# Hymba decoder layer on one core: copy the turned weights first in each step of the attention loop

## The reference

```python
# FoX, per head: scores with a forget term, causal
s = einsum('bqhd,bkhd->bhqk', q, k) * scale
s = s + cum_t[query] - cum_t[key]
a = softmax(where(kpos <= qpos, s, NEG))
o = einsum('bhqk,bkhd->bqhd', a, v)
# NSA: three branches; with 512 tokens all 8 blocks are selected, so the
# selected and the sliding-window branch are both plain causal attention
a = softmax(where(causal, q @ k.T * scale, NEG));  o = a @ v
# the branches are summed with the gates g
```

## Time and profile before

| what | value |
|---|---|
| device time, median of 3 runs | 1250.01 us (1247.60 to 1250.06) |
| the profiled execution: its own time | 1247.07 us |
| its span in the trace | 1245.3 us |
| outside the span | 1.8 us |
| prompt attention, first score to last output copy | 560.8 to 708.7 us |
| one cycle of four steps, NSA half | 9.95 us |
| one cycle of four steps, FoX half | 10.9 us |

### The profile page before, as it was taken

The page is one execution under the profiler, slowest core; times in us unless marked ns, Lnnn a source line. Parts: engine busy times, 40 slices in busy tenths (PEclk is TensorE's granted clock), DMA queues, the critical chain, the costliest instruction groups (busy, mean ns, idle before and its releaser), DMA issues.

```text
span 1245.3 us, 23642 instructions
## 1 busy us (share of the span) xinstructions
PE 1175.5 (94%) x9650; PEld 1079.6 (87%) x9650; DVE 534.9 (43%) x787; ACT 426.3 (34%) x740; POOL 135.6 (11%) x132
## 2 busy tenths in 40 slices
PE   8999999999999999999999756999999999999994
PEld 6999999999998799995655422888999999999994
DVE  4434332343333653545277645545434323343334
ACT  6222222232244632225265523444222212232332
POOL 0110100011111000322011100120110100011110
PEclk9999999999999999999999976999999999999997
DMA  6222223222123223226150062131322232232221
GB/s 270 102 88 81 86 79 108 102 102 75 69 88 110 85 97 143 69 78 217 51 172 2 3 187 102 35 102 35 102 91 78 77 102 96 99 102 77 76 85 69
DMA packets 46002, 117.95 MB, mean 95 GB/s; under 512 B 4154, under 2 KB 21818, under 8 KB 39874
## 3 DMA queue, kind: packets, MB, share of 16 engines
q1 hardware_dynamic: 42738, 110.95, 26.3%
q10 hardware_dynamic: 3184, 5.88, 1.2%
HBM read 110.93 MB, written 7.97 MB: 95 GB/s over the span
## 4 chain that ended last, share of the span: by engine, by line
PE 88%; DVE 7%; ACT 2%; issue 2%; DMA 1%; DVEq 0%; SPq 0%; ACTq 0%
PE ps L1328 75%; PE ps L1455 2%; PE ps L1472 2%; PE ps L1488 2%; PE ps L1503 1%; PE ps L1337 1%; DVE row_max L1077 1%; DVE UT L917 1%; DVE H L921 1%; DVE XL L897 1%; PE ps L1463 1%; PE ps L1630 1%; PE ps L1421 0%; DMA RAW<-in_w_gu 0%; DMA KW<-in_win_k 0%
## 5 line engine op out<-in xcount | busy, mean ns | idle before, releaser
L1328 PE MATMUL ps<-XH,WH 128*128 128x260 f32 x1904 | 389.1, 285 | 8.3 <-DVE XL L897 8.1
L1328 PE MATMUL ps<-XH,WL 128*128 128x260 f32 x1904 | 383.5, 283 | 0.0
L1328 PE MATMUL ps<-XL,WH 128*128 128x260 f32 x1904 | 382.8, 283 | 0.0
L409 ACT CAST WH<-RAW 128x1024 fp32r<-128x1024 f32 (+2 forms) x183 | 174.8, 956 | 530.7 <-PE ps L1328 526.1
L1328 PEld LDWEIGHTS ps<-XH,WH 128*128 128x128 f32 x1904 | 294.6, 188 | 15.0 <-DVE XL L897 12.1
L1328 PEld LDWEIGHTS ps<-XH,WL 128*128 128x128 f32 x1904 | 293.4, 188 | 0.0
L1328 PEld LDWEIGHTS ps<-XL,WH 128*128 128x128 f32 x1904 | 292.7, 188 | 0.0
L412 DVE TENSOR_TENSOR WL<-RAW,WH 128x1024 fp32r<-128x1024 f32 (+2 forms) x183 | 203.7, 1113 | 157.9 <-ACT WH L409 156.6
L1328 PE MATMUL ps<-UL,WH 128*128 128x260 f32 x704 | 141.9, 283 | 0.0
L1328 PE MATMUL ps<-UH,WL 128*128 128x260 f32 x704 | 141.5, 282 | 0.0
L1328 PE MATMUL ps<-UH,WH 128*128 128x260 f32 x704 | 141.3, 282 | 0.0
(11 more groups left out here) (233 smaller groups left out, 934.5 us busy)
## 6 DMA issues: line engine op xcount, KB each, us to landing
RAW<-in_w_gu SPq DMA_DIRECT2D x44, 1024.0 KB, 4.8
RAW<-in_w_down SPq DMA_DIRECT2D x16, 768.0 KB, 4.8
RAW<-in_w_in SPq DMA_DIRECT2D x11, 1024.0 KB, 4.8
RAW<-in_w_down SPq DMA_DIRECT2D x16, 640.0 KB, 4.3
KF<-in_fox_k SPq DMA_DIRECT2D x16, 256.0 KB, 4.4
VF<-in_fox_v SPq DMA_DIRECT2D x16, 256.0 KB, 5.4
RAW<-in_w_out SPq DMA_DIRECT2D x4, 1024.0 KB, 4.9
H<-in_x SPq DMA_DIRECT2D x4, 520.0 KB, 7.2
```

The source lines that it names most:

```text
L409: nc.scalar.copy(WH[:, par, 0:width], RAW[:, slot, j, 0:width]).then_inc(w_hi, 1)
L1328: q = nc.tensor.matmul(ps[:, 2 * slot + half, 0:HALF], w[:, par, cols], x[:, kt0 + kt, half * HALF:(half + 1) * HALF], start=first and kt ...
```

## The change

In every step m from 3 on, except step 14, the copy of the turned pair m-3 stands first: on VectorE before the maximum of pair m, on ScalarE before the exponentials of pair m. In step 14 it stays last, since the burst's results share its banks. No instruction is added or taken away, and TensorE, GpSimd and SyncE keep their order.

```diff
@@ ScalarE, attention() @@
                     if m == 2:
                         ropes_free()
+                    if m >= 3 and m != BURST_AT:
+                        turn_out(act, nc.scalar.copy, 2 * (m - 3) + 1, "att_odd_out")
                     if m < PAIRS:
                         act.wait_ge(sem("att_max"), m + 1)
...
-                    if m >= 3:
+                    if m == BURST_AT:
                         turn_out(act, nc.scalar.copy, 2 * (m - 3) + 1, "att_odd_out")
                     if tiles and m >= pairs_until(tiles[0]) + 4:
                         pair_out(tiles.pop(0))
@@ VectorE, attention() @@
                 for m in range(PAIRS + 3):
+                    if m >= 3 and m != BURST_AT:
+                        turn_out(dve, nc.vector.tensor_copy, 2 * (m - 3), "att_even_out")
                     if m < PAIRS:
                         v, W = 2 * m, P * (unit(2 * m)[3] + 1)
...
-                    if m >= 3:
+                    if m == BURST_AT:
                         turn_out(dve, nc.vector.tensor_copy, 2 * (m - 3), "att_even_out")
```

## The result

The changed kernel took 1235.12 us in the median of 4 runs (1234.73 to 1239.13), before 1250.03 us in 4 runs (1247.60 to 1251.20). The ratio on record is 0.9907 with a 95% interval of 0.9882 to 0.9931. It is an estimate over the executions and not the quotient of the two medians, which is 0.9881. That is 9.4 us by the ratio and 8.9 us by the medians. The change makes the kernel faster by 0.6 to 1.2%.

A forecast was written before the change was run, and what follows sets the result against it. TensorE, busy 94% of the span, was taken as the bound, stalling once per attention cycle for VectorE's copy. Gains of 6.6 and 0.9 us sum to 7.5 us off the 1250.01 us median: 1242.5 us, range 1238.5 to 1247.5.

The forecast's parts named there:

- The ring through S(3): Attention loop, steps with i = 3: S(1) comes 0.64 us earlier, taken as 0.60, 11 times, 6.6 us.
- The end of the loop: After the last S(3): VectorE copies ahead of the last two scalings, so the last T(3) starts 0.9 us earlier.
- Copy first in the other steps: Attention steps with i = 0, 1 and 2: later maxima cost nothing, hidden by the second score buffer; 0.8 to 1.5 us room.
- The clock at the start of the loop: First cycle of the attention loop: the slow clock holds at most 1.5 us, to be won or lost once more.
- After the attention: Stages behind the attention: what follows hangs on its end and moves with it; no gain of its own in the sum.
- The starting point: Whole kernel: the time counted from the three-run median of 1250.01 us, 2.9 us above the profiled execution.
- B: Rival, attention loop: slower hand-overs lengthen the ring, break-even at 0.13 us more for each of five; about 1256 us; chance 0.06.
- C: Rival, attention loop: waits move to a place followed too coarsely, half the gain or more lost; 1246 to 1250 us; chance 0.14.
- D: Rival, attention loop: exponentials do not hold S(1), 1.18 us gained 11 times plus 0.9 us; 1236 us; chance 0.04.
- The clock section's estimate: Whole sum with the first cycle's clock, at most 1.5 us won or lost: a gain of 6 to 9 us.

The follow-up runs named there:

- e3: The changed kernel itself again, in 6 more executions: 1238.86 us against 1247.78 us before, ratio 0.9925.
- e4: Changed kernel with the copies first only in steps with i = 3, last in the others, on both engines: 1250.39 us, ratio 1.0022.
- e6: Changed kernel with VectorE taking the maximum first, then the copy, then reciprocal and scaling; ScalarE's copy still first: 1235.68 us, ratio 0.9905.
- e10: The kernel of e6 once more, in a second set: 1232.96 us, ratio 0.9868.
- e1: Changed kernel with the copy first on VectorE alone, ScalarE's copy last: 1254.73 us against 1247.78 us before, ratio 1.0065.
- e2: Changed kernel with the copy first on ScalarE alone, VectorE's copy last: 1246.55 us, ratio 0.9983.
- e7: Kernel before the change plus 101 matmuls without use in nine gaps between the loop and the output projection: 1244.35 us, ratio 0.9976.

## Why the prediction was wrong

The direction and the mechanism in the loop were right. The sum was too small because it gave every stage outside the loop its old length and counted from a high median. The measured median lies 7.4 us below the forecast. Between the two profiled executions 4.9 us of it can be placed: 3.9 us in the decode stage, 1.5 us of clock in the first cycle, 0.5 us in the ring and at the end of the loop, less 1.0 us in the projection. The other 2.5 us are the starting point. A good part was luck: e3's median of the same kernel, 1238.86 us, lies just inside the range.

- *The ring through S(3).* Forecast: the copy 1.5 us after S(3), the maximum 0.2 us behind it, S(1) waiting about 0.5 us for the exponentials, 0.64 us a cycle. Measured in NSA: 1.50, 0.21, 0.41 and 0.64 us. In FoX the cycle is shorter by 0.64 us too, with a wait of 0.30 us. The step that cut this to 0.60 "since the row starts leave a few hundredths open" was needless and cost 0.4 us.
- *The end of the loop.* Forecast 0.9 us, measured 0.94.
- *Copy first in the other steps.* The forecast called the move in the step with i = 0 free because the maximum behind it has room. e4 shows that this was only half of the account. The move is needed: without it the cycle is 10.24 us. That did not touch the sum, since the change makes both moves.
- *The clock at the start of the loop.* I wrote that the clock holds at most 1.5 us "to be won if it stays up or lost once more", and put nothing into the sum. The first cycle went from 12.44 to 10.28 us, which is 1.52 us more than the ring gives, at a clock of 1.00 where it had been 0.86. But 1.0 us of it was lost ahead of the loop. In e3 the first cycle is 10.80 us at 0.95, and the loop starts 1.7 us later than before:

```profile
560.00:570.00 10.00, 9.34 (x47) 4.66 (x50) 3.54 (x7) 4.87 (x16) 3.00 (x4) 0.66 0.92 316
```

So nothing was the right value for this term over the stages together, and the 1.5 us of the first trace are not a gain to count on. What was missing is the projection ahead of the loop, whose length I took as fixed.
- *After the attention.* This is the step that failed: "What follows hangs on that end, so it moves with it". What follows did move with the end of the loop, but it did not keep its length. The prediction put this term at nothing without having looked at the stage's clock, which was 0.70 in the profiled execution. The stage went from 67.4 to 63.5 us, at 0.79. A stage that swings between 63.5 and 68.1 us for one and the same kernel (e6, e10) belonged in the range of the measured time, and the lower end of 1238.5 had no room for it.
- *The starting point.* I counted from a median of three runs, 1250.01 us. Over 23 executions before has a median of 1247.78 us. 1247.8 less the 8.0 us seen in the rows is 1239.8; e3's median of 1238.86 is 0.9 us below that.

Of the rivals, B (each hand-over grows) did not come: the copy started 0.03 us behind the turning, the exponentials 0.03 us behind the maximum, and S(1) 0.05 us behind the exponentials. B was also priced wrongly. The ring has five links, but only three of them pass from one engine to another, so the change would break even at 0.21 us more for each and not at 0.13, and 0.2 us for each would have cost nothing on this ring. (e1 is slower by another way, through ScalarE's copy.) C did not come: no wait took more than the one forecast. D's time of 1236 us is near the first measurement by chance. Its condition was that the exponentials do not hold S(1), and they held it for 0.41 us. The clock section's estimate of 6 to 9 us covers the 8.0 us of the rows; what it left out are the stages ahead of and behind the loop.

## What to carry to other kernels

When engines wait for each other in turns, find the ring that sets the cycle, and write down the start of each of its members; here that gave 0.64 us of 0.64. A move that shortens one ring had to be made here on each engine and in each step that a neighbouring ring uses; done in part it gained nothing (e2) or made the loop slower (e1, e4). The copy did best between two long instructions and not ahead of both (e6). Look at the granted clock of every stage that follows, also of stages that the change doesn't touch, before giving a range to the time.

## What the runs showed of the hardware

The decode stage ran at a granted clock of 0.68 to 0.79 in the profiled executions without extra matmuls, and at 0.95 to 0.97 with them. Its length went from 67.5 us in before to between 61.4 and 62.4. In the projection the clock fell in the profiled execution of the change (0.83 over 10 us) and not in that of before, with the same instructions, and put off the loop by 1.0 us. The Trainium skill ("TensorE: Matmul & The Clock Gate", "What's actually happening") says that activity is what releases the slow clock; e7 agrees, with 0.97 in place of 0.70. I had expected equal stages to take equal time. That the moment at which the loop ends decides where the falls come is a guess that no run here tells from chance.
